# Moving the feed-forwards' transposing transfers from the sync queue to ScalarE's queue

## What is computed

```
def rms_norm(x, g):
    y = xf * lax.rsqrt(jnp.mean(xf * xf, axis=-1, keepdims=True) + NORM_EPS)
    return (y * g.astype(jnp.float32)).astype(x.dtype)

def swiglu_ffn(h, w_gate, w_up, w_down):      # x: 256 x 1024, w_gate and w_up: 1024 x 2816, w_down: 2816 x 1024
    return (jax.nn.silu(h @ w_gate) * (h @ w_up)) @ w_down
...
x = x + rms_norm_2(swiglu(h, w_gate[l], w_up[l], w_down[l]), post_ffn_g[l])
```

## Time and profile before

| | |
|---|---|
| median of 3 runs | 2033.1 us (2031.86 to 2033.64) |
| the profiled execution | 2033.34 us |
| its span, first to last instruction | 2031.5 us |
| busy: TensorE matmul | 2010.6 us (99%) |
| busy: TensorE weight load | 1653.2 us (81%) |
| busy: VectorE | 1444.2 us (71%) |
| busy: ScalarE | 1122.4 us (55%) |
| granted clock of TensorE | 0.999 |
| DMA queue of the loads | 62.4% of 16 engines' span |

### The profile page before, as it was taken

One profiled execution on the slowest core, in us unless ns is written; L12 is line 12 of the kernel. 1 busy time (PEld: TensorE's weight loads), 2 busy tenths in 40 slices (PEclk: granted clock), 3 DMA queues, 4 the chain that ended last, 5 costly groups with the idle time before them and its releaser, 6 DMA issues.

```text
span 2031.5 us, 24117 instructions
## 1 busy us (share of the span) xinstructions
PE 2010.6 (99%) x9514; PEld 1653.2 (81%) x9514; DVE 1444.2 (71%) x1913; ACT 1122.4 (55%) x1413; POOL 0.2 (0%) x4
## 2 busy tenths in 40 slices
PE   8999999999999999999999999999999999999998
PEld 6888887888888888887888888888888888888887
DVE  6656899776667566899776567966665679667565
ACT  6445657564446455666564446756644457566443
POOL 0000000000000000000000000000000000000000
PEclk9999999999999999999999999999999999999999
DMA  8766764557776875764567767554676675546774
GB/s 281 212 202 183 227 198 145 177 191 206 216 210 215 230 217 170 225 191 146 186 184 216 210 183 212 188 160 142 187 221 202 185 207 190 167 155 187 207 215 122
DMA packets 351377, 394.53 MB, mean 194 GB/s; under 512 B 123792, under 2 KB 259616, under 8 KB 351264
## 3 DMA queue, kind: packets, MB, share of 16 engines
q1 hardware_dynamic: 347168, 381.94, 62.4%
q10 hardware_dynamic: 4096, 11.05, 1.5%
HBM read 365.66 MB, written 1.05 MB: 181 GB/s over the span
## 4 chain that ended last, share of the span: by engine, by line
PE 88%; DVE 5%; ACT 2%; DMA 2%; issue 1%; SPq 1%; ACTq 0%; DVEq 0%
PE ps L620 81%; DVE w_lo L1854 2%; PE ps L691 1%; DVE scratch L2132 1%; PE ps L1202 1%; PE ps L1183 1%; ACT w_hi L1262 1%; DVE x L1904 0%; DMA raw<-in_ffn_w_up 0%; DMA raw<-in_w_in 0%; DVE scratch L2169 0%; DMA raw<-in_w_co 0%; PE ps L714 0%; DVE scratch L2045 0%; DMA x<-in_x 0%
## 5 line engine op out<-in xcount | busy, mean ns | idle before, releaser
L1854 DVE TENSOR_TENSOR w_lo<-raw,w_hi 128x2048 fp32r<-128x2048 f32 x337 | 770.0, 2289 | 216.2 <-ACT w_hi L1262 212.3
L1262 ACT ACTIVATE w_hi<-raw 128x2048 fp32r<-128x2048 f32 x341 | 645.7, 1898 | 466.0 <-PE ps L620 214.2
L620 PE MATMUL ps<-w_hi,hT_hi 128*128 128x512 f32 x2048 | 806.0, 394 | 0.2 <-DVE w_lo L1854 0.2
L620 PE MATMUL ps<-w_lo,hT_hi 128*128 128x512 f32 x2048 | 798.0, 390 | 0.0
L620 PE MATMUL ps<-w_hi,hT_lo 128*128 128x512 f32 x2048 | 774.0, 389 | 0.0
L620 PEld LDWEIGHTS ps<-w_hi,hT_hi 128*128 128x128 f32 x2048 | 385.0, 188 | 83.8 <-issue 5.5
L620 PEld LDWEIGHTS ps<-w_hi,hT_lo 128*128 128x128 f32 x2048 | 384.5, 188 | 80.8
L620 PEld LDWEIGHTS ps<-w_lo,hT_hi 128*128 128x128 f32 x2048 | 385.0, 188 | 76.5
L620 PE MATMUL ps<-w_hi,bT_hi 128*128 128x512 f32 x656 | 257.8, 393 | 1.4 <-DVE bT_lo L1945 1.4
L620 PE MATMUL ps<-w_hi,bT_lo 128*128 128x512 f32 x656 | 255.4, 389 | 0.0
L620 PE MATMUL ps<-w_lo,bT_hi 128*128 128x512 f32 x656 | 255.4, 389 | 0.0
(11 more groups left out here) (293 smaller groups left out, 1120.9 us busy)
## 6 DMA issues: line engine op xcount, KB each, us to landing
raw<-in_w_in SPq DMA_DIRECT2D x160, 512.0 KB, 4.6
raw<-in_ffn_w_down SPq DMA_DIRECT2D x88, 512.0 KB, 4.3
raw<-in_ffn_w_gate SPq DMA_DIRECT2D x87, 512.0 KB, 4.0
raw<-in_ffn_w_up SPq DMA_DIRECT2D x87, 512.0 KB, 5.0
raw<-in_w_gate SPq DMA_DIRECT2D x44, 512.0 KB, 4.0
raw<-in_w_up SPq DMA_DIRECT2D x44, 512.0 KB, 5.0
raw<-in_w_down SPq DMA_DIRECT2D x44, 512.0 KB, 4.4
raw<-in_w_out SPq DMA_DIRECT2D x32, 512.0 KB, 4.2
```

Of the source, the lines that this page charges most:

```text
L620: mm = nc.tensor.matmul(bank(t, half), act[:, tiles[i], t * P:(t + 1) * P], w, start=start and (i, n) == steps[0], stop=stop and (i, n) == ...
L1262: nc.scalar.activation(dst, src, ACT.Copy).then_inc(high_ready, 1)
L1854: V.tensor_tensor(lo, src, flat(hi), ALU.subtract).then_inc(low_ready, 1)
```

## The change

`turn_halves` leaves SyncE's program, with all its calls, and a function of that name stands in ScalarE's `ffn`. It has the same wait and the same two transfers. It is called behind the first `high` after silu in chunks 0 and 1, at the end of `chunk` in chunks 2 to 9, and behind the copy of chunk 9's hidden rows in chunk 10. The mixers' transposing transfers stay with SyncE. TensorE's and VectorE's programs are the same as before.

```diff
-        def turn_halves(L, n, c):
-
-            sp.wait_ge(halves_ready, L.turns(n, c))
-            for t in range(TT):
-                sp.dma_start_transpose(halves_T[:, t, :, :], halves[:, t, :, :].rearrange("p b n -> p (b n)")).then_inc(
-                    halves_turned, 16)
-
-        def ffn(L, n, k0, wg, wu, wd, ffn_ahead=None):
+        def ffn(L, n, k0, wg, wu, wd):
             for kh in range(2):
                 gate_up(L, k0 + kh, kh, wg, wu, 0)
-            if ffn_ahead:
-                turn_halves(*ffn_ahead, NCHUNK - 1)
 
             def chunk(c, k):
                 gate_up(L, k, 0, wg, wu, c)
-                if c > 2:
-                    turn_halves(L, n, c - 2)
                 gate_up(L, k + 1, 1, wg, wu, c)
-                if c == 2:
-                    turn_halves(L, n, 0)
...
             for kh in range(2):
                 gate_up(L, end - 4 + kh, kh, wg, wu, c)
-            turn_halves(L, n, c - 2)
             for i in range(3):
                 down(L, end - 2 + i, wd, c - 2 + i)
-            turn_halves(L, n, c - 1)
...
                     if (n, kh) == (0, 1):
-                        turn_halves(L, 0, NCHUNK - 1)
                         narrow(L, k, d["w_in"], A_LR, RANK)
...
                     if (n, kh) == (0, 1):
-                        turn_halves(*((Layer("B", l - 1), 0) if l else (Layer("A", DEPTH - 1), 1)), NCHUNK - 1)
                         narrow(L, k, d["w_in_2"], B_FF, 8)
...
-        turn_halves(Layer("B", DEPTH - 1), 0, NCHUNK - 1)
...
+            def turn_halves(c):
+
+                act.wait_ge(halves_ready, L.turns(n, c))
+                for t in range(TT):
+                    act.dma_start_transpose(halves_T[:, t, :, :], halves[:, t, :, :].rearrange("p b n -> p (b n)")).then_inc(
+                        halves_turned, 16)
+
...
                 silu(M, k + 1, c)
                 high(M, k + 2 + AHEAD)
+                turn_halves(c)
 
             norm_in(L, j)
             rms_ready(L, j)
             silu(L, k0 + 1, 0, 0)
             high(L, k0 + 1 + AHEAD)
+            turn_halves(0)
             high(L, k0 + 2 + AHEAD)
...
             silu(L, k0 + 3, 1)
             high(L, k0 + 4 + AHEAD)
+            turn_halves(1)
...
             silu(L, end - 3, c, 4)
             hidden(c - 1, hT_hi[:, 0:2, :])
+            turn_halves(c)
             high(L, end - 2 + AHEAD)
             high(L, end - 1 + AHEAD)
             hidden(c, hT_hi[:, 2:4, :])
```

More of the change, by code:

```diff
@@ L510, in _ @@
             L = enter(Layer("A", l))
-            ffn(L, 0, 0, d["ffn1_w_gate"], d["ffn1_w_up"], d["ffn1_w_down"], (Layer("A", l - 1), 1) if l else None)
+            ffn(L, 0, 0, d["ffn1_w_gate"], d["ffn1_w_up"], d["ffn1_w_down"])
             k = U_FFN
```

## The result

The changed kernel takes 2065.66 us (2064.59 to 2066.06, 4 runs) against 2033.37 us of the kernel before on the same chip: ratio 1.0156, 95% interval 1.0144 to 1.0168. It is slower by 32.3 us, where 15.9 were forecast, and lies outside the range. The direction was right; half of the cost was missing.

The account below looks back on a forecast made before the run. The prediction took TensorE's gapless matmuls to bound the feed-forwards. SyncE's removed issues gave 0, mid feed-forward 0, starts 10.95, ends 4.95: 15.9 us on the kernel before, forecast 2049.1 us, range 2038 to 2057.

Parts of the forecast that it names:

- first rival: ScalarE is not held by its issues, so compute behind them starts as before; nothing added, 2033.3 us; chance 0.11.
- favourable reading: Skill's rule that other engine instructions can be queued while a control instruction is worked on; sum 0 instead of 15.9 us.
- third rival: Issues are dearer on ScalarE, or dearer beside SyncE's; between 2057 and 2070.9 us; chance 0.09.
- Step 1: Mid feed-forward, chunks 1 to 9: ScalarE's idle time takes in the 2.50 us of the pair; cost 0.
- Step 3: End of a feed-forward, chunk 10: late join gives five gaps of 0.92 us; 4.95 us with the norm's extra.
- extra 0.35: Where a feed-forward follows a feed-forward, the norm's squares start 1.27 us later, 0.35 over the gap.
- Step 2: Start of a feed-forward: copy of k0 + 5 delays VectorE's join; 2.19 us in five, 0 in A1's second; 10.95 us.
- second rival: Transposes gain from their own queue at the starts: 2031.6 us with free issues; chance 0.03, including anything else faster.

## Why the prediction was half right

**An issue holds ScalarE: right.** The pair takes 2.53 us in the median, and 2.56 to 2.66 at the starts (2.50 taken). Behind none of the 66 pairs does an instruction of ScalarE start before the pair's end, and in the twelve waits, 41.4 us in all, the copy starts 0.10 us after it. The first rival, free issues, falls. So does the favourable reading that stood with it, of a rule of the Trainium skill (Advanced Engine Details and Errata, Sequencer and Instruction Queues): other engine instructions can be read and queued while a control instruction is worked on. For DMA issues on ScalarE this trace shows none that also started. The third rival falls too, although the time went its way: 1.296 us in the median is no dearer issue.

**Step 1, mid feed-forward: right.** 0 forecast, ratio 0.9998 with 54 pairs on ScalarE.

**Step 3, the ends: right.** 4.95 forecast, 5.55 measured with chunk 10 alone moved, by the chain that was worked out. Its extra 0.35 from layer A0 to A1 didn't show, though: the squares of the norm came later by about that much more, but TensorE only by some 0.1, as behind the other ends.

**Step 2, the starts: the step that failed.** "All 2.19 us become a gap", in five feed-forwards, and cost 0 in A1's second. Its chain is right (2.29 with the load held back), but it was one of two chains to the same join, and the other is longer. The prediction costed SyncE's removed issues at nothing, because SyncE waits for slots most of the time. Over the whole run that is so. At this place it isn't: both transfers stood ahead of the load of unit k0 + 7 in SyncE's program, and the load couldn't come before them. With them gone it is under way beside the second transfer, which takes 6.2 us. So the gaps grow by 2.6 to 3.0 instead of 2.19, and there are six: 17.2 us instead of 10.95. The text looked for the effect of an own queue only as a gain, for the transposes to be free of weight packets in SyncE's ring (second rival). It is the other way round. The Trainium skill has a rule that would have asked for this (DMA: Bandwidth & Descriptors, Issuing engines are not separate DMA queues): DMAs run on the same 16 engines and interleave, whichever engine started them. The trace agrees: a median of 4.3 us to landing for the two transfers beside the load, 2.4 without it, both from ScalarE's queue.

**Half-speed matmuls: a term that was missing.** 38 matmuls of 0.43 instead of 0.23 us, 7.6 us. The prediction took a gap to cost its own length. In the table above no gap of 1.91 us or less (start to start) has any behind it; of the 30 from 2.59 us on, 21 have.

**The sum, corrected.** Gaps at the starts 17.2, the matmuls behind them 7.9, ends with what follows 5.9: 31.0 of the 31.3 us between the spans. The starts alone cost 26.6 and the ends alone 5.55, together 32.2 of 32.3.

## What to carry to other kernels

An instruction stream does two things to what stands behind a DMA issue: it delays compute, and it delays the next transfers. When an issue is moved, write down both lists, for the queue that it leaves too: what it kept back there will now run beside it on the same DMA engines. Where a step has several predecessors, work out all their times and not only the one that you came by; and when two turn out close, expect that undoing one shows less than its share (11 us and none here, 20 for both). If urgent work stands behind the issue, putting that work ahead of the prefetching cost nothing measurable here, and closed ten gaps together with the held load.

A caution beside the times: the changed kernel has two streams of transposing transfers, SyncE's for the mixers and ScalarE's for the feed-forwards. The Trainium skill (DMA: Bandwidth & Descriptors, Silent corruption: two transposing streams in flight at once) warns that these must not be in flight together. In this trace at least 42 us lie between the landing of one stream's last transfer and the first issue of the other's; the nearest, from the end of a feed-forward to the mixer behind it:

```profile
797.86 2.53 ACTq L1339 DMA_TRANSPOSE scratch<-scratch  x2
...
843.93 2.63 SPq L492 DMA_TRANSPOSE scratch<-scratch  x2
```

In the three kernels that split the pairs of one feed-forward between the two engines it was as little as 4.5 us.

## What the hardware showed unexpectedly

- A transposing transfer from ScalarE's queue took 2.4 us to landing with the load held back, and 6.2 us where a load of 1 MB was issued 0.3 us behind it from SyncE's. At the first feed-forward, where the load is issued together with the first transfer, it was more: in the kernel with everything first and the load free the join stood idle 7.77 us and the gap there was 7.45. In the kernel before, the load followed the pair at once too (issued at 452.09, the pair at 449.54), but on the same queue and behind both transfers, and TensorE was kept waiting at the first start only. How the DMA engines share themselves between the two queues was not tried.
- What decides whether matmuls run at half speed behind a gap isn't settled. Start to start, a gap of 2.59 us had half speed behind it in the sixth feed-forward with the load held, and gaps of 2.60 in the second and third of the same kernel had none; in the second feed-forward 3.14, 3.22 and 3.27 had none, and 3.21 had eight. The spread of some of these kernels from run to run goes with the granted clock. With everything first and the load free, the run of 2053.55 us has a mean granted clock of 0.998 and those of 2059.89 and 2060.04 have 0.995; 0.003 of a span of 2058 us is 6.2 us, an estimate of the clock lost, and the times differ by 6.3 to 6.5. With chunk 10 on SyncE it is 2057.08 at 0.996 and 2065.19 at 0.992: 8.2 us estimated, 8.1 measured. How many matmuls each of these runs had at half speed isn't known, since one execution of each kernel was profiled.
